# A 256-token, three-block kernel: two feed-forwards end by token tiles, a norm's last square moves to VectorE, and the gate row is multiplied in fp32r

## What is computed

```python
for i in range(DEPTH):          # 2
    x = x + 0.5 * swiglu(rms_norm(x, ffn1_norm[i]), ...)
    h = rms_norm(x, mix_norm[i])
    x = x + (moba_mixer(h, ...) if i % 2 == 0 else mamba2_mixer(h, ...))
    x = x + 0.5 * swiglu(rms_norm(x, ffn2_norm[i]), ...)
# second block
mod = silu(c) @ w_ada + b_ada
shift, scale, gate = split(mod, 3)
h = rms_norm(x, norm_g) * (1 + scale) + shift
...
x = x + gate * (m @ w_out)
return rms_norm(x, final_g)
```

## Time and profile before

| | us |
|---|---|
| median of 3 runs | 1322.38 (1322.37 to 1322.51) |
| the profiled execution | 1323.11 |
| its span | 1321.3 |
| TensorE busy | 1308.9 (99%) |
| VectorE busy | 1079.3 (82%) |
| ScalarE busy | 713.4 (54%) |
| GpSimd busy | 210.1 (16%) |

### The profile page before, as it was taken

The page is one execution under the profiler, slowest core; times in us unless marked ns, Lnnn a source line. Parts: engine busy times, 40 slices in busy tenths (PEclk is TensorE's granted clock), DMA queues, the critical chain, the costliest instruction groups (busy, mean ns, idle before and its releaser), DMA issues.

```text
span 1321.3 us, 20183 instructions
## 1 busy us (share of the span) xinstructions
PE 1308.9 (99%) x7751; PEld 1106.1 (84%) x7751; DVE 1079.3 (82%) x1592; ACT 713.4 (54%) x840; POOL 210.1 (16%) x193
## 2 busy tenths in 40 slices
PE   9999999999999999999999999999999999999998
PEld 7888888888888888888899988788888888888886
DVE  6977788868999789998786999769777767878587
ACT  6444455665444454444465688854444466558553
POOL 2400001102000010000000035300000011664940
PEclk9999999999999999999999999999999999999999
DMA  8655555528577754776544565475655554654541
GB/s 274 223 191 190 190 178 205 190 80 305 193 262 265 243 183 149 266 234 223 180 160 160 179 210 181 138 254 166 209 195 197 194 173 160 201 172 141 175 150 57
DMA packets 158445, 254.29 MB, mean 192 GB/s; under 512 B 8800, under 2 KB 99248, under 8 KB 156704
## 3 DMA queue, kind: packets, MB, share of 16 engines
q1 hardware_dynamic: 155136, 232.68, 52.1%
q0 software_dynamic: 2576, 18.45, 4.0%
q10 hardware_dynamic: 656, 2.11, 0.5%
HBM read 252.12 MB, written 1.08 MB: 192 GB/s over the span
## 4 chain that ended last, share of the span: by engine, by line
PE 96%; ACT 1%; DVE 1%; POOL 1%; issue 1%; DMA 0%; SPq 0%; POOLq 0%; DVEq 0%; ACTq 0%
PE psum L712 12%; PE psum L718 12%; PE psum L705 12%; PE psum L737 5%; PE psum L736 5%; PE psum L735 5%; PE psum L2003 4%; PE psum L2005 4%; PE psum L2004 4%; PE psum L438 2%; PE psum L439 2%; PE psum L445 2%; PE psum L473 2%; PE psum L481 2%; PE psum L475 2%; PE psum L504 2%
## 5 line engine op out<-in xcount | busy, mean ns | idle before, releaser
L390 ACT ACTIVATE w_hi<-raw 128x2048 fp32r<-128x2048 f32 (+1 forms) x220 | 419.8, 1910 | 316.4 <-PE psum L718 121.5
L402 DVE TENSOR_TENSOR w_lo<-raw,w_hi 128x2048 fp32r<-128x2048 f32 x219 | 507.3, 2337 | 100.2 <-ACT w_hi L390 98.7
L839 DVE STREAM_TRANSPOSE hidT<-hid 32x128 f32<-32x128 f32 x704 | 213.1, 303 | 22.1
L705 PE MATMUL psum<-w_hi,hT 128*128 128x512 f32 x704 | 174.6, 390 | 0.1
L718 PE MATMUL psum<-w_lo,hT 128*128 128x512 f32 x704 | 173.9, 389 | 0.0
L712 PE MATMUL psum<-w_hi,hT 128*128 128x512 f32 x704 | 173.9, 389 | 0.0
L712 PEld LDWEIGHTS psum<-w_hi,hT 128*128 128x128 f32 x704 | 132.2, 188 | 27.4
L718 PEld LDWEIGHTS psum<-w_lo,hT 128*128 128x128 f32 x704 | 132.2, 188 | 27.4
L705 PEld LDWEIGHTS psum<-w_hi,hT 128*128 128x128 f32 x704 | 131.9, 188 | 27.8 <-ACT w_hi L1009 0.8
L786 ACT ACTIVATE silu_g<-psum,rstd 128x256 f32<-128x256 f32 x88 | 36.9, 471 | 113.2 <-PE psum L718 107.6
L2003 PE MATMUL psum<-w_hi,hT 128*128 128x512 f32 x224 | 88.8, 397 | 0.0
(11 more groups left out here) (407 smaller groups left out, 2186.1 us busy)
## 6 DMA issues: line engine op xcount, KB each, us to landing
raw<-in_ffn_w_down SPq DMA_DIRECT2D x88, 512.0 KB, 4.9
raw<-in_ffn_w_gate SPq DMA_DIRECT2D x87, 512.0 KB, 3.8
raw<-in_ffn_w_up SPq DMA_DIRECT2D x87, 512.0 KB, 5.1
raw<-in_w_in SPq DMA_DIRECT2D x72, 512.0 KB, 4.5
raw<-in_ssm_w_in SPq DMA_DIRECT2D x48, 512.0 KB, 4.6
raw<-in_attn_w_qkv SPq DMA_DIRECT2D x24, 512.0 KB, 4.6
ada_in<-in_w_ada POOLq DMA_DIRECT2D x8, 1536.0 KB, 7.2
raw<-in_ssm_w_out SPq DMA_DIRECT2D x16, 512.0 KB, 4.3
```

Source lines behind the costliest of these rows:

```text
L390: act.activation(to, src, ACT.Copy).then_inc(sem("hi_ready"), 1)
L402: dve.tensor_tensor(to, src, hi.bitcast(F32), ALU.subtract).then_inc(sem("lo_ready"), 1)
L705: pe.matmul(psum[:, banks[t], :], hT_hi[:, k, t * P:(t + 1) * P], hi[:, kk, :], start=k == 0, stop=False)
L839: dve.transpose(to[:, :, :, 32 * a:32 * (a + 1)], src[:, :, :, 32 * b:32 * (b + 1)])\
```

## The change

1. `last_down` of ffn1_1 and ffn2_1 runs its four parts as (t, h) = 00, 01, 10, 11, and the adds and squares follow that order.
2. In norms 4 and 6 ScalarE squares three parts and VectorE the last (`last_squares_dve`), starting its sum from GpSimd's mean square of the first half. ScalarE scales both halves of tile 0 and the second half of tile 1; VectorE scales the first half of tile 1 only.
3. Norm 4's transposes go to banks 4 to 7, two k tiles in each. The gate row goes to banks 2 and 3, the turned columns to bank 0. TensorE's order is gate row, tile 0's transposes, turned columns, tile 1's transposes.
4. The gate row is split into an fp32r high part (ScalarE) and low part (VectorE) inside ffn1_1, and multiplied with an fp32r copy of the ones in two passes for each half. VectorE's copy of it comes after the second and third weight split of the mixer, and chunk 1 of the mixer waits for it.
5. In norm 6 ScalarE writes hT_hi of k = 0, 1, 4, 5 straight from PSUM (`hi_at_once`); VectorE modulates those tiles after it and subtracts.

```diff
+        last_ms = keep("last_ms", [P, 4])
+        ones_r = keep("ones_r", [P, P], R32)
...
+        ada_hi = zoned("pair", "ada_hi", [P, D], R32)
+        ada_lo = zoned("pair", "ada_lo", [P, D], R32, offset=4 * D)
...
-        last_ms = r("last_ms", [P, 4])
...
-            banks = {0: (2, 3, 4, 6, 7), 2: (4, 5, 6, 7, 2), 4: (2, 7, 4, 6, 5), 5: (2, 3, 4, 5, 6), 6: (2, 5, 4, 6, 7)}.get(n, (2, 3, 4, 6, 5))
+            banks = {0: (2, 3, 4, 6, 7), 2: (4, 5, 6, 7, 2), 4: (4, 5, 6, 7), 5: (2, 3, 4, 5, 6), 6: (2, 5, 4, 6, 7)}.get(n, (2, 3, 4, 6, 5))
+            if len(banks) == 4:
+                return banks[k // 2]
...
+
+            return k if k < 2 and n != 4 else k | 1
...
-                squares(act, n)
-                act.wait_ge(sem("rstd"), rstd_count(n, 0))
-                for cs in HALVES:
-                    act.activation(xn[:, 0, cs], x[:, 0, cs], ACT.Copy, scale=rstd[:, 0:1]).then_inc(sem("xn_0"), 1)
+                squares(act, n, [(0, 0), (1, 0), (0, 1)])
+                for t, cs in ((0, HALVES[0]), (0, HALVES[1]), (1, HALVES[1])):
+                    act.wait_ge(sem("rstd"), rstd_count(n, t))
+                    act.activation(xn[:, t, cs], x[:, t, cs], ACT.Copy, scale=rstd[:, t:t + 1]).then_inc(sem("xn_act"), 1)
...
-            pool.wait_ge(sem("sumsq"), 4 * n + 2)
-            order(pool.tensor_scalar(meansq[:, :], sumsq[:, 0, :], 1.0, EPS, ALU.mult, ALU.add))
-            for t in range(TT):
-                ts = slice(t, t + 1)
-                pool.wait_ge(sem("sumsq"), 4 * n + 2 + t + 1)
-                order(pool.tensor_tensor(meansq[:, ts], meansq[:, ts], sumsq[:, 1, ts], ALU.add))
-                pool.tensor_tensor(rstd[:, ts], meansq[:, ts], neg_half[:, ts], ALU.pow).then_inc(sem("rstd"), 1)
+            done = 4 * n
+            pool.wait_ge(sem("sumsq"), done + 1)
+            order(pool.tensor_scalar(meansq[:, 0:1], sumsq[:, 0, 0:1], 1.0, EPS, ALU.mult, ALU.add))
+            pool.wait_ge(sem("sumsq"), done + 2)
+            order(pool.tensor_tensor(meansq[:, 0:1], meansq[:, 0:1], sumsq[:, 1, 0:1], ALU.add))
+            pool.tensor_tensor(rstd[:, 0:1], meansq[:, 0:1], neg_half[:, 0:1], ALU.pow).then_inc(sem("rstd"), 1)
+            pool.wait_ge(sem("sumsq"), done + 3)
+            pool.tensor_scalar(meansq[:, 1:2], sumsq[:, 0, 1:2], 1.0, EPS, ALU.mult, ALU.add).then_inc(sem("last_low"), 1)
+            pool.wait_ge(sem("sumsq"), done + 4)
+            pool.tensor_tensor(rstd[:, 1:2], last_ms[:, 0:1], neg_half[:, 0:1], ALU.pow).then_inc(sem("rstd"), 1)
...
+        def last_squares_dve(dve, n):
+
+            dve.wait_ge(sem("x_added"), 4 * n)
+            dve.wait_ge(sem("last_low"), BY_TILE.index(n) + 1)
+            last = x[:, 1, HALVES[1]]
+            dve.tensor_tensor_reduce(xn[:, 1, HALVES[1]], last, last, 1.0 / D, meansq[:, 1:2], ALU.mult, ALU.add,
+                                     last_ms[:, 0:1]).then_inc(sem("sumsq"), 1)
...
-                for cs in HALVES:
-                    dve.tensor_scalar(xn[:, 1, cs], x[:, 1, cs], rstd[:, 1:2], None, ALU.mult).then_inc(sem("xn_1"), 1)
+                cs = HALVES[0]
+                dve.tensor_scalar(xn[:, 1, cs], x[:, 1, cs], rstd[:, 1:2], None, ALU.mult).then_inc(sem("xn_dve"), 1)
...
-        def norm_pe(pe, n, deferred, xn_before=0):
...
-                for t in range(TT):
+                i = BY_TILE.index(n)
+                for t in ts:
                     for k in range(KD):
-                        if k % 4 == 0:
-                            pe.wait_ge(sem(f"xn_{t}"), xn_before + k // 4 + 1)
+                        if k == 0 and t:
+                            pe.wait_ge(sem("xn_dve"), i + 1)
+                        elif k % 4 == 0:
+                            pe.wait_ge(sem("xn_act"), 3 * i + (3 if t else k // 4 + 1))
...
+        TOKENWISE = ("ffn1_1", "ffn2_1")
+
+        def last_parts(f):
+
+            if f in TOKENWISE:
+                return [(t, h) for t in range(TT) for h in range(2)]
+            return [(t, h) for h in range(2) for t in range(TT)]
...
-                for h in range(2):
-                    cs = slice(512 * h, 512 * h + 512)
-                    for t in range(TT):
-                        for k in range(2):
-                            to = psum[:, 4 + 2 * t + h, :]
-                            a, b = (part[:, k, t * P:(t + 1) * P] for part in hidT_parts[c % 2])
-                            pe.matmul(to, a, hi[:, k, cs], start=False, stop=False)
-                            pe.matmul(to, a, lo[:, k, cs], start=False, stop=False)
-                            m = pe.matmul(to, b, hi[:, k, cs], start=False, stop=k == 1)
-                        m.then_inc(sem("unit_used" if h and t else "down_part"), 1)
+                for part, (t, h) in enumerate(last_parts(f)):
+                    to, cs = psum[:, 4 + 2 * t + h, :], slice(512 * h, 512 * h + 512)
+                    for k in range(2):
+                        a, b = (both[:, k, t * P:(t + 1) * P] for both in hidT_parts[c % 2])
+                        pe.matmul(to, a, hi[:, k, cs], start=False, stop=False)
+                        pe.matmul(to, a, lo[:, k, cs], start=False, stop=False)
+                        m = pe.matmul(to, b, hi[:, k, cs], start=False, stop=k == 1)
+                    m.then_inc(sem("unit_used" if part == 3 else "down_part"), 1)
...
+            if before_last:
+                before_last(act)
...
         def gate2_pe(pe):
             pe.wait_ge(sem("ada"), ADA_PIECES * KD)
+            pe.wait_ge(sem("ada_parts"), 3)
             for h in range(2):
-                m = pe.matmul(psum[:, h, :], ones, ada[:, 2 * D + 512 * h:2 * D + 512 * (h + 1)],
-                              start=True, stop=True)
+                cs = slice(512 * h, 512 * (h + 1))
+                pe.matmul(psum[:, 2 + h, :], ones_r[:, :], ada_hi[:, cs], start=True, stop=False)
+                m = pe.matmul(psum[:, 2 + h, :], ones_r[:, :], ada_lo[:, cs], start=False, stop=True)
             m.then_inc(sem("mod_ready"), 1)
+
+        def gate2_parts_act(act):
+
+            act.activation(ones_r[:, :], ones, ACT.Copy).then_inc(sem("ada_parts"), 1)
+            act.wait_ge(sem("ada"), ADA_PIECES * KD)
+            act.activation(ada_hi[:, :], ada[:, 2 * D:3 * D], ACT.Copy).then_inc(sem("ada_parts"), 1)
+
+        def gate2_parts_dve(dve):
+            dve.wait_ge(sem("ada_parts"), 2)
+            dve.tensor_tensor(ada_lo[:, :], ada[:, 2 * D:3 * D], ada_hi[:, :].bitcast(F32), ALU.subtract)\
+               .then_inc(sem("ada_parts"), 1)
...
-                    m = pe.matmul(psum[g:g + MOD_TILE, 3, j * MOD_TILE:(j + 1) * MOD_TILE],
+                    m = pe.matmul(psum[g:g + MOD_TILE, 0, j * MOD_TILE:(j + 1) * MOD_TILE],
...
         def ssm_pe(pe):
             gate2_pe(pe)
+            norm_pe(pe, 4, False, (0,))
             mod_pe(pe)
-            norm_pe(pe, 4, False)
+            norm_pe(pe, 4, False, (1,))
...
+                elif c:
+                    pe.wait_ge(sem("mod_read"), 2)
...
         def ssm_dve(dve):
+            last_squares_dve(dve, 4)
+            norm_dve(dve, 4, None, False)
+            mod_dve(dve)
+            early, late = second_and_third("ssm_xbc")
+            hT_lo_tiles(dve, 4, ("mix_norm", KD), range(4))
+            split_lo(dve, early)
+            hT_lo_tiles(dve, 4, ("mix_norm", KD), range(4, KD))
+            split_lo(dve, late)
             gate2_dve(dve)
-            mod_dve(dve)
-            norm_dve(dve, 4, ("mix_norm", KD), False, second_and_third("ssm_xbc"))
...
-                act.wait_ge(sem("xT"), 6 * KD + last_of_bank(k) + 1)
+                act.wait_ge(sem("xT"), 6 * KD + last_of_bank(6, k) + 1)
                 act.activation(h_tmp[:, k, :], turned_x(6, k), ACT.Identity, bias=mod_cols[:, k:k + 1],
                                scale=gain2[:, k:k + 1]).then_inc(sem("h_act"), 1)
 
             def hi_of_h(k):
-                act.wait_ge(sem("h_act" if k & 2 else "h_dve"), 2 * (k // 4) + k % 2 + 1)
+                act.wait_ge(sem("h_act"), 2 * (k // 4) + k % 2 + 1)
                 act.activation(hT_hi[:, k, :], h_tmp[:, k, :], ACT.Copy).then_inc(sem("hT_hi"), 1)
 
+            def hi_at_once(k):
+                act.wait_ge(sem("xT"), 6 * KD + last_of_bank(6, k) + 1)
+                act.activation(hT_hi[:, k, :], turned_x(6, k), ACT.Identity, bias=mod_cols[:, k:k + 1],
+                               scale=gain2[:, k:k + 1]).then_inc(sem("hT_hi"), 1)
+
             for k in (0, 4):
-                hi_of_h(k)
+                hi_at_once(k)
+                hi_at_once(k + 1)
                 modulated(k + 2)
-                hi_of_h(k + 1)
                 modulated(k + 3)
                 hi_of_h(k + 2)
...
+            early, late = second_and_third("in2")
+            last_squares_dve(dve, 6)
...
-                dve.wait_ge(sem("xT"), 6 * KD + last_of_bank(k) + 1)
+                dve.wait_ge(sem("hT_hi"), 6 * KD + last_of_bank(6, k) + 1)
```

(43 more changed lines are left out.)

24 lines of the change are left out of this document (12 added, 12 removed).

## The result

| | before | after |
|---|---|---|
| median, us (9 runs each) | 1322.46 (1322.37 to 1322.63) | 1326.28 (1326.04 to 1326.49) |
| the profiled execution, us | 1323.11 | 1326.28 |
| its span, us | 1321.3 | 1324.5 |
| mean granted clock | 0.999 | 0.998 |

The changed kernel is 3.8 us slower: ratio 1.0029, 95% interval 1.002 to 1.0037. The forecast was 0.8 us faster, and 1326.28 lies outside the range of 1320.7 to 1322.8.

The account below looks back on a forecast made before the run. TensorE, busy 1308.9 of 1321.3 us, was taken to bound the kernel. Gains of 0.5 us at the first seam and 0.3 at the second summed to 0.8, taking median 1322.38 to 1321.6 us, range 1320.7 to 1322.8.

Parts of the forecast that it names:

- TensorE is gapless behind both seams, so it should stay: After the seams ffn1_1 to state-space stage and ffn2_1 to in2, the 0.8 us gain was to persist.
- (c): Rival: new first-seam holes lower TensorE's clock, cancelling the gain or giving 1327.4 us over one state-space unit; 2%.
- The sum of the change's own work: Both seams together: 0.5 + 0.3 = 0.8 us gained, median 1321.6 us.
- the first place: Last ffn1_1 feed-forward matmul to first state-space matmul: 0.5 us gained, bounds 0.25 and 0.6.
- Gate row: First seam: four fp32r matmuls 0.23 us apart, 0.91 us in place of 1.81, at most 0.90 saved.
- Both forecast holes: First seam: TensorE gets two new holes, 0.2 and 0.1 us, around the first four transposes of tile 0.
- VectorE's subtraction of the gate row (L1114): First seam: 1.22 us of work pushes the first add by 0.9 us and delays the second by 0.35.
- VectorE's square: Tile 1's wide square with its sum: taken as 0.85 us, 1.16 at the dear end.
- (a): Rival: tile 1's chain is dear at both seams, square 1.16 and pow 1.00; median 1322.6 us; 12%.
- Second place: Last ffn2_1 matmul to first in2 matmul: 0.3 us gained, bounds 0 and 0.4; no wait before tile 0's transposes.
- The pow beside the `lb_top` and `lb_e` steps: Second seam: kept at 0.57 us; at 1.00 that seam would lose 0.1 and the sum be 0.4.
- (b): Rival: the gain is given back, an earlier TensorE waiting for weight loads bound by wall clock; median 1322.4 us; 9%.

Follow-up runs that it names:

- experiment 1: Changed kernel with everything behind the kept tiles placed 128 bytes further, again 128 bytes above a multiple of 256: 1321.54 us, ratio 0.9992.
- the residue restored: Changed kernel with the working zone's start back at 128 modulo 256 (start modulo 256 is the residue), run twice: 1321.54 us, then 1321.68 us.
- the norms alone: Changed kernel with the zone at 128 modulo 256 and the gate row back in one fp32 product without its halves: 1322.14 us, ratio 0.9998.

## Why the prediction was wrong

**The failed step** is the sentence under the sum: "TensorE is gapless behind both seams, so it should stay". It took for granted that a stretch with the same instructions takes the same time. I costed every operation, wait and queue of the diff, and gave its first two lines, the two `keep` calls, no cost, for they are no work. They were the dearest lines of the diff: 4.7 us (experiment 1 against the changed kernel), five times what all its work brings in. No rival named it, and the 2% for slower was the share of (c) "and what I overlooked". The profile before could have said little: every 512-wide product with weights ran at the fast relation, so no slow row was there to be seen. The diff could, since `WORK` is worked out from what is kept ahead of it.

**The sum of the change's own work was right.** 0.8 us forecast, 0.9 measured with the residue restored (1321.54 and 1321.68, forecast 1321.6). That it agrees so closely is in part luck: the first place brought 0.07 less than forecast, and the first unit of in2 0.12 that no term of the sum had. Its steps, one by one:

- Gate row: four matmuls 0.23 us apart, as forecast, 0.92 us for 1.81.
- First place: 0.41 gained for 0.48 (rounded to 0.5). Both forecast holes are there. The first is 0.2 us (661.95 against 661.53 + 0.23 = 661.76). The second, of 0.1, lies inside tile 0's eight transposes, which take 1.11 us to the next start and took 0.97 with the norms alone, where TensorE arrives later. There is none between the tiles. What was mis-sized is the end: the first mixer matmul waits, as forecast, for ScalarE's first hT, and that step takes 0.47 us where I took 0.42, which is what L2184 takes. The column turning takes 1.26 us for 1.23.

```profile
664.77 0.47 ACT L558 ACTIVATE hT<-psum,cols 128x256 fp32r<-128x256 f32 x1 [0.79 <-PE psum L639]
```

- VectorE's subtraction of the gate row (L1114) was to delay tile 0's second add by 0.35 us. It did not: that add ends at 659.07, less the shift of 2.12 us at 656.95, as before. The copies begin when forecast, since they wait for ScalarE's third square, so this error did not reach the sum.
- VectorE's square: 0.85 us from its start to GpSimd's pow (1062.37 to 1063.22), the 0.85 that I took. The dear end of 1.16 was (a), and it did not come.
- Second place: 0.32 for 0.3, and 0.12 more in the first unit of in2. No wait ahead of tile 0, as forecast. The transposes take 2.24 in place of 2.06 us, which holds the wait for tile 1 (some 0.2 us, forecast 0.3), and behind them TensorE waits 1.08 us for VectorE's hT where it waited 0.93.
- The pow beside the `lb_top` and `lb_e` steps took 0.55 us. They ran from 1063.05 to 1063.5 and it from 1063.22. The Trainium skill (SBUF — State Buffer, "Who interferes with whom") would have it wait; with steps of 8 columns no wait shows in this trace (0.55 us, against 0.57 before), and the sum was right to keep 0.57.
- (b) and (c): TensorE has no new wait for a load; the clock granted is 1.00 around both places before and after, and the fillers take 1.98 us in both. A span that "does not shrink by what the seams do" I had named as the mark of (b); that mark appeared, and (b) was still wrong. It asked for a wait, and TensorE idled 1.0 us less than before.

## What to carry to other kernels

When a diff adds, drops or resizes a tile that others are placed behind, write down which starts move and by how much modulo 256 before costing anything else, and compare the mean of one matmul by tile, at one shape and line, in the two profiles. In a kernel that TensorE bounds, a few nanoseconds on each of thousands of matmuls outweigh a whole seam; when a total moves against what the changed stretches show, line up the starts of the same instruction in both traces and look where the shift grows.
